# Modulation sums as one-column products on TensorE, squares of x added on VectorE, and x loaded between the weight tiles

## The chip, the cores and the metric

The kernel runs on one core of a Trainium2 chip. The time is the device time of one execution in microseconds (us); less is better. A core has five engines with a program each: TensorE (PE in the profile, its weight loads PEld), VectorE (DVE), ScalarE (ACT), GpSimd (POOL) and SyncE (SP, which here issues every DMA). They meet only through semaphores.

## The reference

Two transformer blocks on 512 rows of width 1024, all in float32. The change is in what stands ahead of the first block's projections. With x of 512 rows and a vector c of 1024 numbers it computes

```python
mod = c @ w_ada[l] + b_ada[l]                    # (1024) @ (1024, 3072)
shift, scale, gate = jnp.split(mod, 3, axis=-1)
h = _rmsnorm(x, norm_g[l]) * (1.0 + scale[:, None, :]) + shift[:, None, :]
proj = h @ w_in[l]                               # (512, 1024) @ (1024, 6152)
# _rmsnorm(x, g) = x * rsqrt(mean(x * x, axis=-1) + 1e-6) * g
# behind it: stick-breaking attention, forgetting attention, gates, and
# x = x + gate[:, None, :] * (merged @ w_out[l]), then the second block
# (differential attention and convolution, cross attention, conv FFN)
```

`shift` and `scale` are needed before the first projection can start; `gate` much later. `w_ada` has 12 MB, of which 8 MB are for `shift` and `scale`.

## The kernel before, in words

Activations are kept transposed: features on the 128 partitions, the 512 rows along the free dimension, in 8 pieces (`X[:, k, :]`, `HH[:, k, :]`). Weights come in "units" of 128x1024 float32 (512 KB) in a fixed order (`UNITS`), through a ring of four buffers `RAW`. A projection's unit is split in two parts: ScalarE copies it to `WH` (rounded to float32r), GpSimd computes the rest `WL = RAW - WH` in four pieces; TensorE makes three products of each piece (high by high, high by low, low by high).

The first 16 units are `w_ada`: `("ada", 1, k)` for scale and then `("ada", 0, k)` for shift, k = 0..7; a unit holds the 128 rows 128k.. of the matrix and 1024 columns. Behind them come `("av", 0..3)`, the first projection's weights. SyncE's program (`sync_program`) issues the loads in the order of `UNITS`; the load of unit j waits until the buffer's last user, unit j-4, is done. For an `ada` unit that is the signal `s_mod`, for others `s_wh` and `s_wl`.

Each engine's order of work is written out by hand. Up to the first projection it is, before the change:

- **VectorE** (`mod_step`): for each `ada` unit `ma = ma + raw * c[k]`, one pass over 128x1024, where c[k] is one number per partition. Eight passes leave a tile whose sum over the partitions is the product with c. Among the last passes stand the norm's small steps (`root_cols`, `root_inverse`, `diag`, `spread_out`).
- **TensorE** (`mod_end`): eight products of a 128x128 piece of `ma` (the stationary operand) with a column of ones, so that the sum over the partitions comes out with one feature per partition. TensorE also adds the squares of x over the features (`sums`: 8 pieces, each a high and a low part, with a constant matrix), and spreads the norm's factor over the partitions (`spread`).
- **ScalarE**: square of x piece by piece, its high part, the root, the `WH` of the four `av` units, and then `HH[:, k, :]`.
- **GpSimd**: the low parts of the eight squares, then the `WL` of the `av` units.

The loads begin with the parameters (`par_sb`, which hold c), half of x, `raw(0)`, the other half, the constants, then three units. After the 16th `ada` unit VectorE makes `mod_out(0, 1)`, and then for each k a tile `tm`, from which ScalarE makes `HH[:, k, :]` and VectorE `HL[:, k, :]`; TensorE's `vproj("a", ...)` uses them k by k.

In the profile an engine's instructions all carry the line of the helper that emits them: L135 matmul, L142 activation, L145 `tt`, L148 `stt`, L153 `ts`, L156 `cp`, L168 DMA. They are told apart by the tiles.

Of the kernel before, what the change touches and what calls it, by code (L numbers as in the profile page):

```python
# [15 lines left out]
P = 128  # L16
# [234 lines left out]
def build(nc, args):  # L251
# [5 lines left out]
    def at(name, shape, dt, offset=None):  # L257
        nb = int(np.prod(shape[1:])) * (2 if dt == BF16 else 4)
        if offset is None:
            offset = off[0]  # L260
            off[0] += (nb + 31) // 32 * 32
        assert offset + nb <= 229344, (name, offset + nb)
        return nc.alloc_sbuf_tensor_at(name, list(shape), dt, offset=offset)
# [62 lines left out]
    SZ = [at(f"sz{i}", [P, T], F32) for i in range(2)]  # L326
    FT = at("ft", [104, T], F32R)
    MA = at("ma", [P, U], F32, a1)
    MA2 = at("ma2", [P, U], F32, a1 + 4096)

    off[0] = a1
    RB = at("rb", [P, T], F32)
# [56 lines left out]
    def sig(name, step=1):  # L389
        signals.append(Signal(name, step))  # L390
        return signals[-1]
# [8 lines left out]

    s_wh, s_wl, s_unit = sig("s_wh"), sig("s_wl"), sig("s_unit")

    s_sq, s_sqha, s_sqhd, s_sqlp, s_sqld, s_sum = (
        sig(n) for n in ("s_sq", "s_sqha", "s_sqhd", "s_sqlp", "s_sqld", "s_sum"))
    s_add, s_root, s_sqrt, s_spread = sig("s_add"), sig("s_root"), sig("s_sqrt"), sig("s_spread")

    s_conr, s_mk, s_mod, s_modp, s_modc, s_gain = (
        sig(n) for n in ("s_conr", "s_mk", "s_mod", "s_modp", "s_modc", "s_gain"))

    s_ht, s_hh, s_hl = sig("s_ht"), sig("s_hh"), sig("s_hl")  # L410
    s_vh, s_vl, s_qh, s_ql, s_kh, s_kl, s_sz = (
# [56 lines left out]
    def tensor_program(pe):  # L468
# [37 lines left out]
        def sums(key, b, ones, p, hs, ls, first, last, n=T):  # L506
            pe.wait_ge(hs, *key)
            pe.mm(PS[b][:, 0:n], con_r(ones), SQh[p][:, 0:n], first, False)
            pe.wait_ge(ls, *key)
            pe.mm(PS[b][:, 0:n], con_r(ones), SQl[p][:, 0:n], False, last).then_inc(*s_sum.up(*key))  # L510
# [17 lines left out]
            bank[b] = (s_modc, (part,))  # L528

        pe.wait_ge(s_conr, 0)
        for k in range(KC):
            sums(("x", k), 7, "o1024", k % 2, s_sqha, s_sqlp, k == 0, k == KC - 1)
        mod_end(1, 0, MA)
        bank[7] = (s_root, ("x", "mult"))
        spread("x", 7, TM[2])
        bank[7] = (s_root, ("x", "out"))
        mod_end(0, 1, MA2)

        def vproj(br, nm, gen):  # L540
            for u in range(4):
# [591 lines left out]
    def lam(a, b):  # L1133
        return LM[:, a:b]
# [38 lines left out]
    def scalar_program(act):  # L1173
# [19 lines left out]

        for k in range(KC):
            act.wait_ge(l_x if k < 4 else l_xb, 0)
            if k == 7:
                act.wait_ge(s_sqlp, "x", 0)
            square(TM[k % 7][:, :], ("x", k), X[:, k, :])
            if k >= 2:
                act.wait_ge(s_sum, "x", k - 2)  # L1200
            act.wait_ge(s_sq, "x", k)
            act.fn(SQh[k % 2][:, :], TM[k % 7][:, :], ACT.Copy).then_inc(*s_sqha.up("x", k))
        act.wait_ge(l_con, 0)
        root("x", ncol("x"))
        for j in range(N_ADA, N_ADA + RING):
# [75 lines left out]

        act.wait_ge(l_mem, 0)
        act.fn(MSQ[:, :, :], MEMT[:, :, :], ACT.Square).then_inc(*s_sq.up("mem"))
        act.wait_ge(s_modp, 0)
        vproj("a", "av", VAh)
        qk_high("a", 0, "q")
        root("mem", ncol("mem", 2))
# [354 lines left out]
    def vector_program(dve):  # L1642
# [54 lines left out]
        dve.wait_ge(l_cont, 0)  # L1697
        dve.cp(conr[:, :], CONT[:, :]).then_inc(*s_conr.up(0))

        def mod_step(part, k, ma):  # L1700
            j = PLACE["ada", part, k]
            dve.wait_ge(l_raw[j % RING], j)
            dve.wait_ge(l_par, 0)
            if k == 0:
                dve.ts(ma[:, :], RAW[j % RING][:, :], pcol("c", k), ALU.mult).then_inc(*s_mod.up(part, k))
            else:
                dve.wait_ge(s_mod, part, k - 1)
                dve.stt(ma[:, :], RAW[j % RING][:, :], pcol("c", k), ma[:, :], ALU.mult,
                        ALU.add).then_inc(*s_mod.up(part, k))

        def mod_out(part, b):
            dve.wait_ge(s_modp, part)
            dve.tt(sm[:, 8 * part:8 * part + 8], PS[b][:, 0:8], prow("b_ada", 8, 8 * part),
                   ALU.add).then_inc(*s_modc.up(part))

        for k in range(KC):
            mod_step(1, k, MA)
        for k in range(KC):
            mod_step(0, k, MA2)
            if k == 1:  # L1720
                mod_out(1, 0)
                root_cols("x", 7, TM[1], ("x", 7))
                root_inverse("x")
            if k == 3:
                diag("x", TM[2], ncol("x"), "x")
            if k == 4:
                spread_out("x", 7, SZ[1][:, :])
        dve.wait_ge(l_msk, 0)
        dve.cp(MK[:, 0:512], MKR[:, 0:512]).then_inc(*s_mk.up(0))
        dve.cp(MK[:, 512:768], MKR[:, 512:768]).then_inc(*s_mk.up(1))  # L1730
        dve.wait_ge(s_modc, 1)
        dve.ts(sm[:, 8:16], sm[:, 8:16], 1.0, ALU.add).then_inc(*s_gain.up("one"))
        dve.wait_ge(s_gain, "one")
        dve.tt(sm[:, 8:16], sm[:, 8:16], prow("norm_g", 8), ALU.mult).then_inc(*s_gain.up("g"))
        mod_out(0, 1)
        dve.wait_ge(s_gain, "g")
        dve.wait_ge(s_root, "x", "out")
        dve.wait_ge(s_modc, 0)
        dve.wait_ge(s_sqlp, "x", 7)
        for k in range(KC):  # L1740
            t = TM[(3 + k) % 7]
            if k == 7:
# [608 lines left out]
    def pool_program(pool):  # L2351
# [15 lines left out]
        def parts(l, src, h, key, s_l):  # L2367
            pool.tt(l, src, f32(h), ALU.subtract).then_inc(*s_l.up(*key))

        for k in range(KC):  # L2370
            pool.wait_ge(s_sqha, "x", k)
            if k >= 2:
                pool.wait_ge(s_sum, "x", k - 2)
            parts(SQl[k % 2][:, :], TM[k % 7][:, :], SQh[k % 2][:, :], ("x", k), s_sqlp)
        for j in range(N_ADA, N_ADA + RING):
            low(UNITS[j])
        for name in UNITS[N_ADA:PLACE["ak", 0] + 1]:
# [63 lines left out]
    def sync_program(sp):  # L2441
        def raw(j):
            s = j % RING
            if j >= RING:
                name = UNITS[j - RING]
                if name[0] == "ada":
                    sp.wait_ge(s_mod, name[1], name[2])
                else:
                    sp.wait_ge(s_wh, name)
                    sp.wait_ge(s_wl, name)  # L2450
            sp.dma(RAW[s][:, :], units[j]).then_inc(*l_raw[s].up(j))
# [6 lines left out]
                sp.dma(gate_tile(k, x)[:, :], gate_w[k, :, T * x:T * x + T]).then_inc(*l_gate[x].up(k))  # L2458

        sp.dma(par_sb[:, :], par).then_inc(*l_par.up(0))  # L2460
        sp.dma(X[:, 0:4, :], xin[:, 0:4, :]).then_inc(*l_x.up(0))
        raw(0)
        sp.dma(X[:, 4:8, :], xin[:, 4:8, :]).then_inc(*l_xb.up(0))
        sp.dma(CONT[:, :], con[:, 0:CO + 8]).then_inc(*l_cont.up(0))
        sp.dma(con_raw[:, :], con[:, CO:NCON]).then_inc(*l_con.up(0))
        for j in range(1, RING):
            raw(j)
        sp.dma(MKR[:, :], msk).then_inc(*l_msk.up(0))
        def keep(n):
            sp.wait_ge(s_gl, n)  # L2470
            sp.dma(kept[n, :, :], GE[n % 3][:, :]).then_inc(*l_kept[n % 3].up(n))
# [12 lines left out]
        for j in range(RING, len(UNITS)):  # L2484
            done = UNITS[j - 2 * RING] if j >= 2 * RING else None
            if done and done[0] == "g":
                keep(2 * (done[1] % 8) + done[1] // 8)
            for k, first in enumerate((0, 2, 5, 7, 10, 12, 14, 15)):
                if j == b0 + first:
                    gate(k)  # L2490
            if j == PLACE["oa", 0] + RING + 3:
                for n in range(6):
                    back(n)
            if j == PLACE["oa", 0] + 2 * RING:
                sp.wait_ge(s_pv, "b", 7)
                sp.dma(X[:, :, :], xin).then_inc(*l_x2.up(0))
            for u in range(3):
                if j == PLACE["ob", u] + 2 * RING + 1:
                    for n in range(4 * u + 6, min(4 * u + 10, 16)):
                        back(n)  # L2500
            if j == PLACE["wo", 0] + 2 * RING:
                sp.wait_ge(s_unit, ("ob", 3))
                sp.dma(CT[:, :].bitcast(I32), posin).then_inc(*l_pos.up(0))
                sp.dma(lam(0, 256), lamin).then_inc(*l_lam.up(0))
            if j == N_ADA + RING:
                sp.wait_ge(s_modc, 0)
                sp.dma(MEMT[:, :, :], memin).then_inc(*l_mem.up(0))
            if j == PLACE[gate_unit(5)] + 2 * RING:
                sp.wait_ge(s_mxl, 3)
                sp.dma(kept_m[0, :, :], f32(MEMh[:, :, :]).rearrange("p k m -> p (k m)")).then_inc(*l_mout[0].up(0))  # L2510
                sp.dma(kept_m[1, :, :], f32(MEMl[:, :, :]).rearrange("p k m -> p (k m)")).then_inc(*l_mout[1].up(0))
            if j == PLACE["dk", 3] + 2 * RING + 1:
                sp.wait_ge(s_unit, ("dk", 3))
                for x, t in enumerate((MTh, MTl)):
                    sp.wait_ge(l_mout[x], 0)
                    sp.dma(f32(t[:, :, :]).rearrange("p k m -> p (k m)"), kept_m[x, :, :]).then_inc(*l_min[x].up(0))
            if j == PLACE["cv", 3, 1] + 2 * RING:
                sp.wait_ge(s_pv, "d", 7)
                for x, (p0, p1) in enumerate(((0, 6), (6, 8))):
                    sp.wait_ge(s_kv, p1 - 1)  # L2520
                    sp.dma(KV[:, p0:p1, :], KVT[:, p0:p1, :]).then_inc(*l_kv[x].up(0))
            raw(j)
# [119 lines left out]
```

## Time and profile before

| | us |
|---|---|
| median of 3 runs | 1446.15 (1442.12 to 1448.85) |
| the profiled execution, its own time | 1445.63 |
| its span, first to last instruction | 1443.8 |
| TensorE matmul busy | 1310.3 (91% of the span) |
| VectorE busy | 793.9 (55%) |
| ScalarE busy | 576.1 (40%) |
| GpSimd busy | 747.8 (52%) |

The span is 1.8 us shorter than the execution's own time. Busy shares are averages over the whole span. The change touches only the stretch ahead of the first projection, some 50 us, and that stretch has to be read by itself.
### The profile page before, as it was taken

The page shows a single profiled execution, that of the slowest core. Times are in us where ns is not written, and L with a number is a line of the kernel's source. Part 1 is how long each engine was busy: PE and PEld are TensorE (multiplying, and loading weights), DVE is VectorE, ACT ScalarE, POOL GpSimd, SP SyncE. Part 2 cuts the span into 40 slices and gives each one's busy share as a digit, 9 for nine tenths or more (in the row PEclk, how much of TensorE's full clock was granted, in tenths as well). Part 3 has the DMA queues.
Part 4 walks back from the last instruction along what each step waited for, and adds up shares of the span by engine and source line. Part 5 has one row for each costly group of instructions (what it writes and reads, how often), then busy time and mean ns, then how long its engine had stood idle before and what let it go on. Part 6 is the DMA issues. An engine that isn't in the chain of part 4 may idle for free.

```text
span 1443.8 us, 17006 instructions
## 1 busy us (share of the span) xinstructions
PE 1310.3 (91%) x6164; PEld 1065.3 (74%) x6164; DVE 793.9 (55%) x1339; ACT 576.1 (40%) x926; POOL 747.8 (52%) x866
## 2 busy tenths in 40 slices
PE   3789999989999899999978788998999999999996
PEld 2567878867888777787656677787878888888874
DVE  5646767423334248796675553775336733661554
ACT  3354555435555236222433453543334423332331
POOL 4353434432333466476233366842556976884771
PEclk9989999999999999999999799999999999999998
DMA  8531223212323642132111334321231333233321
GB/s 298 175 103 51 74 66 124 90 65 92 102 87 111 222 134 95 61 95 95 59 59 44 114 109 144 105 86 44 66 95 61 108 110 97 93 102 101 89 74 58
DMA packets 41699, 142.80 MB, mean 99 GB/s; under 512 B 4624, under 2 KB 5008, under 8 KB 40464
## 3 DMA queue, kind: packets, MB, share of 16 engines
q1 hardware_dynamic: 41616, 141.71, 30.3%
q8 instruction: 49, 0.80, 0.2%
q14 instruction: 34, 0.28, 0.1%
HBM read 131.21 MB, written 8.39 MB: 97 GB/s over the span
## 4 chain that ended last, share of the span: by engine, by line
PE 77%; DVE 12%; ACT 6%; issue 2%; DMA 1%; POOL 0%; SPq 0%; DVEq 0%; ACTq 0%; POOLq 0%
PE ps L135 76%; DVE tm L145 3%; ACT wh L142 2%; ACT tm L142 2%; DVE ma L148 1%; PE ps L139 1%; ACT L142 1%; DVE tm L148 1%; DMA con_raw<-con 1%; ACT hh L142 1%; DVE sql L145 0%; DVE ac L148 0%; DVE x L148 0%; DVE tm L153 0%; DVE stat L159 0%
## 5 line engine op out<-in xcount | busy, mean ns | idle before, releaser
L145 POOL TENSOR_TENSOR wl<-raw,wh 128x256 fp32r<-128x256 f32 x804 | 677.9, 876 | 621.0 <-ACT wh L142 618.8
L142 ACT ACTIVATE wh<-raw 128x1024 fp32r<-128x1024 f32 x201 | 212.2, 1058 | 506.1 <-PE ps L135 494.0
L135 PE MATMUL ps<-hh,wh 128*128 128x512 f32 x872 | 344.7, 395 | 2.8 <-DVE cb L145 1.6
L135 PE MATMUL ps<-hl,wh 128*128 128x512 f32 x872 | 340.6, 391 | 0.0
L135 PE MATMUL ps<-hh,wl 128*128 128x512 f32 x872 | 340.4, 390 | 0.0
L135 PEld LDWEIGHTS ps<-hh,wh 128*128 128x128 f32 x872 | 164.7, 189 | 39.0 <-DVE cb L145 2.4
L135 PEld LDWEIGHTS ps<-hh,wl 128*128 128x128 f32 x872 | 164.2, 188 | 35.1
L135 PEld LDWEIGHTS ps<-hl,wh 128*128 128x128 f32 x872 | 164.4, 189 | 33.5 <-issue 0.5
L148 DVE SCALAR_TENSOR_TENSOR tm<-cb,par_sb,tm 128x512 f32<-128x512 f32 x88 | 87.5, 994 | 50.8 <-ACT tm L142 47.5
L145 DVE TENSOR_TENSOR tm<-tm,tm 128x512 f32<-128x512 f32 (+3 forms) x106 | 91.0, 862 | 35.3 <-ACT tm L142 32.4
L142 ACT ACTIVATE tm<-tm 128x512 f32<-128x512 f32 (+3 forms) x109 | 54.5, 532 | 87.2 <-DVE tm L148 81.6
L145 DVE TENSOR_TENSOR x<-ps,x 128x512 f32<-128x512 f32 x40 | 27.5, 688 | 101.7 <-PE ps L135 101.6
L142 ACT ACT_TABLE_LOAD x50 | 64.2, 1283 | 28.5 <-DVE stat L153 15.2
L135 PE MATMUL ps<-zh,wh 128*128 128x512 f32 x176 | 69.9, 397 | 2.3 <-DVE zh L156 2.3
L135 PE MATMUL ps<-zl,wh 128*128 128x512 f32 x176 | 69.3, 394 | 0.8 <-POOL zl L145 0.8
L135 PE MATMUL ps<-zh,wl 128*128 128x512 f32 x176 | 69.6, 395 | 0.0
L142 ACT ACTIVATE tm<-ps,stat 128x256 f32<-128x256 f32 (+3 forms) x80 | 40.8, 516 | 46.9 <-DVE stat L153 46.8
L148 DVE SCALAR_TENSOR_TENSOR ac<-cpf,par_sb,ac 128x512 f32<-128x512 f32 x60 | 56.5, 941 | 1.6
L159 DVE TENSOR_REDUCE stat<-ps 128x1 f32<-128x256 f32 (+3 forms) x80 | 37.6, 470 | 30.5 <-PE ps L135 30.4
L145 DVE TENSOR_TENSOR cb<-ps,rb 128x512 f32<-128x512 f32 x44 | 30.1, 684 | 28.6 <-PE ps L135 28.5
L142 ACT ACTIVATE tm<-cb,par_sb 128x512 f32<-128x512 f32 x44 | 31.3, 712 | 29.7 <-DVE cb L145 29.6
L135 PE MATMUL ps<-wh,hh 128*128 128x512 f32 x96 | 38.8, 404 | 4.0 <-ACT hh L142 4.0
(316 smaller groups left out, 2414.7 us busy)
## 6 DMA issues: line engine op xcount, KB each, us to landing
raw<-units SPq DMA_DIRECT2D x217, 512.0 KB, 3.5
kept<-ge SPq DMA_DIRECT2D x16, 256.0 KB, 2.0
tm<-kept SPq DMA_DIRECT2D x16, 256.0 KB, 3.7
tm<-gate_w SPq DMA_DIRECT2D x12, 256.0 KB, 4.1
x<-xin SPq DMA_DIRECT2D x2, 1024.0 KB, 6.7
x<-xin SPq DMA_DIRECT2D x1, 2048.0 KB, 12.1
out<-x SPq DMA_DIRECT2D x8, 256.0 KB, 2.2
kv<-kvt SPq DMA_DIRECT2D x1, 1536.0 KB, 7.3
```

Source lines behind the costliest of these rows:

```text
L135: return self.none if self.e is None else self.e.matmul(out, lhs, rhs, start=start, stop=stop, skip_group_check=skip)
L139: return self.none if self.e is None else self.e.transpose(out, in_, ident)
L142: return self.none if self.e is None else self.e.activation(out, in_, func, **kw)
L145: return self.none if self.e is None else self.e.tensor_tensor(out, a, b, op)
L148: return self.none if self.e is None else self.e.scalar_tensor_tensor(out, a, s, b, op0, op1)
L159: return self.none if self.e is None else self.e.tensor_reduce(out, in_, AX_X, op, **kw)
```

## The change

- `mod_step`, `MA2` and two of the three `mod_end` go. In their place TensorE multiplies each `ada` unit directly: eight products per unit, each a 128x128 piece of `RAW` (stationary) with the column c[k] of the parameters (one moving column), summed over k in PSUM (`ada(part, k)`). The signal `s_ada`, given by the last of the eight, is what the reload of the buffer waits for.
- The squares of x are added on VectorE (`add_square`): pieces 0 to 6 into one tile, and the sum and piece 7 are each split in high and low there. TensorE makes four products instead of sixteen, in the middle of the `ada` units. ScalarE keeps only the squares, GpSimd has nothing to do there.
- Units 0 to 3 are loaded earlier, the halves of x between them, and the mask `MKR` comes later, behind unit 17.

```diff
-        pe.wait_ge(s_conr, 0)
+        def ada(part, k):
+            s = PLACE["ada", part, k] % RING
+            pe.wait_ge(l_par, 0)
+            pe.wait_ge(l_raw[s], PLACE["ada", part, k])
+            for f in range(8):
+                last = pe.mm(PS[part][:, f:f + 1], RAW[s][:, f * 128:(f + 1) * 128], pcol("c", k), k == 0 and f == 0,
+                             k == 7, skip=True)
+            last.then_inc(*s_ada.up(part, k))
+
         for k in range(KC):
-            sums(("x", k), 7, "o1024", k % 2, s_sqha, s_sqlp, k == 0, k == KC - 1)
-        mod_end(1, 0, MA)
-        bank[7] = (s_root, ("x", "mult"))
-        spread("x", 7, TM[2])
-        bank[7] = (s_root, ("x", "out"))
-        mod_end(0, 1, MA2)
+            ada(1, k)
+        bank[1] = (s_modc, (1,))
+        for k in range(KC):
+            ada(0, k)
+            if k == 2:
+                pe.wait_ge(s_conr, 0)
+                sums(("x", 6), 7, "o1024", 0, s_sqhd, s_sqld, True, False)
+                sums(("x", 7), 7, "o1024", 1, s_sqhd, s_sqld, False, True)
+                bank[7] = (s_root, ("x", "mult"))
+            if k == 6:
+                spread("x", 7, TM[5])
+                bank[7] = (s_root, ("x", "out"))
+        bank[0] = (s_modc, (0,))
...
         for k in range(KC):
             act.wait_ge(l_x if k < 4 else l_xb, 0)
-            if k == 7:
-                act.wait_ge(s_sqlp, "x", 0)
-            square(TM[k % 7][:, :], ("x", k), X[:, k, :])
-            if k >= 2:
-                act.wait_ge(s_sum, "x", k - 2)
-            act.wait_ge(s_sq, "x", k)
-            act.fn(SQh[k % 2][:, :], TM[k % 7][:, :], ACT.Copy).then_inc(*s_sqha.up("x", k))
+            if k >= 3:
+                act.wait_ge(s_add, "x", k - 2)
+            square(square_tile(k)[:, :], ("x", k), X[:, k, :])
...
         for k in range(KC):
-            mod_step(1, k, MA)
-        for k in range(KC):
-            mod_step(0, k, MA2)
-            if k == 1:
-                mod_out(1, 0)
-                root_cols("x", 7, TM[1], ("x", 7))
-                root_inverse("x")
-            if k == 3:
-                diag("x", TM[2], ncol("x"), "x")
-            if k == 4:
-                spread_out("x", 7, SZ[1][:, :])
+            add_square("x", k, (None, None))
+        root_cols("x", 7, TM[6], ("x", 7))
+        root_inverse("x")
+        diag("x", TM[5], ncol("x"), "x")
         dve.wait_ge(l_msk, 0)
         dve.cp(MK[:, 0:512], MKR[:, 0:512]).then_inc(*s_mk.up(0))
         dve.cp(MK[:, 512:768], MKR[:, 512:768]).then_inc(*s_mk.up(1))
+        mod_out(1, 1)
...
+        spread_out("x", 7, SZ[1][:, :])
+        mod_out(0, 0)
...
                 if name[0] == "ada":
-                    sp.wait_ge(s_mod, name[1], name[2])
+                    sp.wait_ge(s_ada, name[1], name[2])
```

`add_square` stands in the kernel before already, for later norms; it adds `t0 = t0 + t` for f = 1..6 and splits `t0` and the last square in two parts each.

TensorE's program in the kernel before, from the low part of the last square to the second product of the first projection (`ma` and `ma_125` hold the sums for scale and shift, `tm_68` the norm's diagonal; `x8` are the eight pieces):

```order
L135 MATMUL ps<-sql_84,conr 128x512
L135 MATMUL ps<-con_raw,ma 128x1 x8
L135 MATMUL ps<-tm_68,con_raw 128x512
L135 MATMUL ps<-con_raw,ma_125 128x1 x8
L135 MATMUL ps<-wh_53,hh 128x512
L135 MATMUL ps<-wl_57,hh 128x512
```

The same place in the changed kernel, from the third shift unit on (`raw_49` to `raw_52` are the ring's four buffers, `par_sb` holds the column c[k]):

```order
L135 MATMUL ps<-par_sb,raw_51 128x1 x8
L135 MATMUL ps<-sqh_81,conr 128x512
L135 MATMUL ps<-sql_83,conr 128x512
L135 MATMUL ps<-sqh_82,conr 128x512
L135 MATMUL ps<-sql_84,conr 128x512
L135 MATMUL ps<-par_sb,raw_52 128x1 x8
L135 MATMUL ps<-par_sb,raw_49 128x1 x8
L135 MATMUL ps<-par_sb,raw_50 128x1 x8
L135 MATMUL ps<-par_sb,raw_51 128x1 x8
L135 MATMUL ps<-tm_71,con_raw 128x512
L135 MATMUL ps<-par_sb,raw_52 128x1 x8
L135 MATMUL ps<-wh_53,hh 128x512
```

Two groups of eight one-column products stood ahead of the first projection; now sixteen do, eleven ahead of this piece's second row and five behind it.

SyncE's program at the very start, as the difference from before (-) to after (+):

```order
 L168 DMA par_sb<-par 128x374
+L168 DMA raw_49<-units 128x1024
+L168 DMA raw_50<-units 128x1024
 L168 DMA x<-xin 128x2048
-L168 DMA raw_49<-units 128x1024
-L168 DMA x<-xin 128x2048
+L168 DMA raw_51<-units 128x1024
+L168 DMA raw_52<-units 128x1024
 L168 DMA cont<-con 128x776
 L168 DMA con_raw<-con 128x400
```

Two weight units now stand ahead of the first half of x, and only the parameters ahead of them; the second half of x goes behind the constants.

## Rows read from the trace of the kernel before

**Rows 1.** The page: span, and the chain that ended last by engine.

```profile
span 1443.8 us, 17006 instructions
...
PE 77%; DVE 12%; ACT 6%; issue 2%; DMA 1%; POOL 0%; SPq 0%; DVEq 0%; ACTq 0%; POOLq 0%
```

**Rows 2.** Chain in order of time, 0 to 110 us: start, duration, what.

```profile
25.63 2.11 DVE ma L148
27.74 0.04 issue
27.78 3.59 PE ps L135 x16
...
43.54 1.29 DVE ma L148
44.85 4.69 DMA raw<-units
49.56 0.25 ACT wh L142
...
54.20 40.14 PE ps L135 x167
```

**Rows 3.** Timeline from 12 us: start, duration, engine, line, out<-in, [idle <-releaser].

```profile
12.95 0.63 PE L135 MATMUL ps<-sql,conr 128*128 128x512 f32 x1
12.96 0.33 PEld L135 LDWEIGHTS ps<-sqh,conr 128*128 128x128 f32 x1
13.00 32.18 SPq L168 DMA_DIRECT2D raw<-units  x16
13.07 14.65 DVE L148 SCALAR_TENSOR_TENSOR ma<-raw,par_sb,ma 128x1024 f32<-128x1024 f32 x7
13.38 0.63 PE L135 MATMUL ps<-sqh,conr 128*128 128x512 f32 x1
...
27.78 3.49 PEld L135 LDWEIGHTS ps<-con_raw,ma 128*128 128x128 f32 x16 [0.79 <-DVE ma L148]
27.78 3.57 PE L135 MATMUL ps<-con_raw,ma 128*128 128x1 f32 x16 [0.29 <-DVE ma L148]
...
38.08 2.05 PE L135 MATMUL ps<-tm,con_raw 128*128 128x512 f32 x2 [6.72 <-DVE tm L145]
...
44.87 3.57 PE L135 MATMUL ps<-con_raw,ma 128*128 128x1 f32 x16 [4.75 <-DVE ma L148]
...
55.86 0.63 PE L135 MATMUL ps<-wh,hh 128*128 128x512 f32 x1
...
56.28 0.63 PE L135 MATMUL ps<-wl,hh 128*128 128x512 f32 x1
```

**Rows 4.** Instructions writing `ma` or reading it, 20 to 32 us: ns min/median/max.

```profile
L135 PEld LDWEIGHTS ps<-con_raw,ma x16: 288/333/333, 27.8 to 30.9; 128*128 128x128 f32 x16
```

**Rows 5.** Timeline of TensorE at the fast pace, 58 us and 481 us.

```profile
58.70 0.40 PE L135 MATMUL ps<-wl,hh 128*128 128x512 f32 x1
...
58.93 0.40 PE L135 MATMUL ps<-wh,hl 128*128 128x512 f32 x1
...
481.57 1.84 PE L135 MATMUL ps<-con_raw,ma 128*128 128x1 f32 x16
483.27 0.48 PE L135 MATMUL ps<-vah,wh 128*128 128x512 f32 x1
```

**Rows 6.** DMA issues, 0 to 60 us: KB each, median us from issue to landing.

```profile
raw<-units SPq DMA_DIRECT2D x24, 512.0 KB, 4.5
x<-xin SPq DMA_DIRECT2D x2, 1024.0 KB, 6.7
...
par_sb<-par SPq DMA_DIRECT2D x1, 187.0 KB, 2.4
```

**Rows 7.** The page's DMA issues over the whole span.

```profile
raw<-units SPq DMA_DIRECT2D x217, 512.0 KB, 3.5
```

**Rows 8.** Stretches of 2 us: PE, PEld, DVE, ACT, POOL busy, PEclk, DMA share, GB/s.

```profile
4.00:6.00 2.00, 0.00 (x0) 0.00 (x0) 0.00 (x0) 0.00 (x0) 0.00 (x0) 1.00 0.96 395
...
14.00:16.00 2.00, 1.45 (x4) 0.64 (x3) 1.90 (x2) 1.91 (x4) 1.67 (x2) 1.00 1.03 401
...
22.00:24.00 2.00, 1.22 (x2) 0.50 (x2) 1.90 (x2) 0.69 (x2) 2.00 (x2) 1.00 0.77 225
...
40.00:42.00 2.00, 0.12 (x1) 0.00 (x0) 1.84 (x2) 0.00 (x0) 0.00 (x0) 1.00 0.90 324
```

**Rows 9.** VectorE by group, the whole span.

```profile
L145 DVE TENSOR_TENSOR tm<-tm,tm 128x512 f32<-128x512 f32 x81 | 80.2, 995 | 13.5 <-ACT tm L142 10.6
...
L145 DVE TENSOR_TENSOR sql<-tm,sqh 128x512 fp32r<-128x512 f32 x12 | 11.6, 968 | 0.4
...
L156 DVE CAST sqh<-tm 128x512 fp32r<-128x512 f32 x12 | 8.3, 688 | 1.0 <-ACT tm L142 0.8
```

More of the change, by code:

```diff
@@ L328, in build @@
     MA = at("ma", [P, U], F32, a1)
-    MA2 = at("ma2", [P, U], F32, a1 + 4096)
     off[0] = a1
@@ L401, in build @@
     s_wh, s_wl, s_unit = sig("s_wh"), sig("s_wl"), sig("s_unit")
-    s_sq, s_sqha, s_sqhd, s_sqlp, s_sqld, s_sum = (
-        sig(n) for n in ("s_sq", "s_sqha", "s_sqhd", "s_sqlp", "s_sqld", "s_sum"))
+    s_sq, s_sqhd, s_sqld, s_sum = sig("s_sq"), sig("s_sqhd"), sig("s_sqld"), sig("s_sum")
     s_add, s_root, s_sqrt, s_spread = sig("s_add"), sig("s_root"), sig("s_sqrt"), sig("s_spread")
-    s_conr, s_mk, s_mod, s_modp, s_modc, s_gain = (
-        sig(n) for n in ("s_conr", "s_mk", "s_mod", "s_modp", "s_modc", "s_gain"))
+    s_conr, s_mk, s_ada, s_mod, s_modp, s_modc, s_gain = (
+        sig(n) for n in ("s_conr", "s_mk", "s_ada", "s_mod", "s_modp", "s_modc", "s_gain"))
     s_ht, s_hh, s_hl = sig("s_ht"), sig("s_hh"), sig("s_hl")
@@ L1283, in scalar_program @@
         act.fn(MSQ[:, :, :], MEMT[:, :, :], ACT.Square).then_inc(*s_sq.up("mem"))
-        act.wait_ge(s_modp, 0)
         vproj("a", "av", VAh)
@@ L1698, in vector_program, with mod_out @@
         dve.cp(conr[:, :], CONT[:, :]).then_inc(*s_conr.up(0))
-        def mod_step(part, k, ma):
-            j = PLACE["ada", part, k]
-            dve.wait_ge(l_raw[j % RING], j)
+        def mod_out(part, b):
             dve.wait_ge(l_par, 0)
-            if k == 0:
-                dve.ts(ma[:, :], RAW[j % RING][:, :], pcol("c", k), ALU.mult).then_inc(*s_mod.up(part, k))
-            else:
[L1707 to L1712, printed above, removed]
+            if part == 2:
+                dve.wait_ge(s_modp, 2)
+            else:
+                dve.wait_ge(s_ada, part, 7)
             dve.tt(sm[:, 8 * part:8 * part + 8], PS[b][:, 0:8], prow("b_ada", 8, 8 * part),
@@ L1734, in vector_program @@
         dve.tt(sm[:, 8:16], sm[:, 8:16], prow("norm_g", 8), ALU.mult).then_inc(*s_gain.up("g"))
-        mod_out(0, 1)
+        spread_out("x", 7, SZ[1][:, :])
+        mod_out(0, 0)
         dve.wait_ge(s_gain, "g")
@@ L1738, in vector_program @@
         dve.wait_ge(s_modc, 0)
-        dve.wait_ge(s_sqlp, "x", 7)
         for k in range(KC):
@@ L2368, in parts @@
             pool.tt(l, src, f32(h), ALU.subtract).then_inc(*s_l.up(*key))
[L2370 to L2374, printed above, removed]
         for j in range(N_ADA, N_ADA + RING):
@@ L2460, in sync_program @@
         sp.dma(par_sb[:, :], par).then_inc(*l_par.up(0))
+        raw(0)
+        raw(1)
         sp.dma(X[:, 0:4, :], xin[:, 0:4, :]).then_inc(*l_x.up(0))
-        raw(0)
-        sp.dma(X[:, 4:8, :], xin[:, 4:8, :]).then_inc(*l_xb.up(0))
+        raw(2)
+        raw(3)
         sp.dma(CONT[:, :], con[:, 0:CO + 8]).then_inc(*l_cont.up(0))
         sp.dma(con_raw[:, :], con[:, CO:NCON]).then_inc(*l_con.up(0))
-        for j in range(1, RING):
-            raw(j)
-        sp.dma(MKR[:, :], msk).then_inc(*l_msk.up(0))
+        sp.dma(X[:, 4:8, :], xin[:, 4:8, :]).then_inc(*l_xb.up(0))
         def keep(n):
@@ L2504, in sync_program @@
                 sp.dma(lam(0, 256), lamin).then_inc(*l_lam.up(0))
+            if j == N_ADA + 2:
+                sp.dma(MKR[:, :], msk).then_inc(*l_msk.up(0))
             if j == N_ADA + RING:
```

## The prediction, made before the changed kernel ran

> **What bounds the kernel now.** The page comes first: TensorE makes up 77% of the chain that ended last, VectorE 12% [rows 1]. That is the whole span, and the change touches its first 50 us, so the next view is the chain in order of time from 0 to 110 us. There TensorE isn't the engine that sets the end. The chain runs over VectorE's passes on `ma` (the last of the first eight at 25.63), over one group of 16 one-column passes on TensorE (27.78, 3.59 us), over VectorE's passes again up to 44.83, then over the load of the last `av` unit (44.85, 4.69 us) and ScalarE's copy of it at 49.56. From 54.20 on TensorE has 167 matmuls in one piece [rows 2]. So what the first stage costs the kernel is read off one event: the moment from which TensorE runs the first projection without a gap, 54.20. All that follows hangs on that, and shifts with it.
>
> The timeline shows why VectorE takes so long: seven passes in 14.65 us, of which the last takes 2.11 where one of the second eight takes 1.29 [rows 2, 3]. GpSimd is busy beside the long ones (2.00 of 2 us at 22 to 24) and idle beside the short ones (0.00 at 40 to 42) [rows 8]. The load isn't the limit: the DMA engines moved 395 to 401 GB/s at 4 to 6 and 14 to 16 us, and 225 at 22 to 24, when a free buffer was what they lacked [rows 8].
>
> **The clock.** PEclk reads 1.00 in these stretches [rows 8], since no change is on record ahead of 58.42. The pace says something else: consecutive 512-column passes start 0.43 us apart at 12.95 and 13.38 [rows 3], against 0.23 at 58.70 and 58.93 [rows 5]. So TensorE runs at 1.2 GHz in the stage that the change alters, and at 2.4 GHz from 58.4 on.
>
> **What goes.** VectorE's 16 passes over `raw` and the two groups of `ma` products leave the path. GpSimd's eight low parts and ScalarE's eight copies go too; neither is in the chain.
>
> **What comes on TensorE.** The new product has exactly the form of the old one in `mod_end`: a 128x128 float32 piece loaded, one column moved. Its price is in the trace. Eight products are 16 passes, loaded in 3.49 us with the last load taking 0.288, hence (3.49 - 0.288) / 15 = 0.2135 us from one pass to the next [rows 3, 4]. At 2.4 GHz, at 481.57, the 16 take until 483.27: 1.70 us, 0.106 a pass [rows 5]. The price is that of the weight load; the single column costs nothing beside it. A unit so costs 16 x 0.2135 = 3.42 us at the slow clock, against 1.29 to 2.11 us on VectorE. That is the heart of the forecast: the change takes the sum from an engine that needs 1.3 us for a unit to one that needs 3.4, and all 16 units stand in TensorE's own order ahead of the first projection.
>
> The Trainium skill (TensorE: Matmul & The Clock Gate, section "LDWEIGHTS (loading the stationary operand)") gives a load as columns divided by 1.2 GHz, which is 107 ns for 128 columns. By that a unit would cost 1.7 us at the low clock. The trace has 213 ns a pass for this float32 form [rows 3, 4], twice the page's figure, and the measurement decides.
>
> **The sum**, as the time at which the 16th unit is done:
> - Start. The parameters landed 2.4 us after their issue at about 0.74 [rows 6], so 3.1 is the earliest. They and the first unit are 0.7 MB; 0.4 MB/us from about 3 us [rows 8] puts the landing at 4.7. The late end is 6.5: a first half of x of 1 MB, behind the parameters, had 6.7 us as median from issue [rows 6], and this load is half of that. I take 4.7.
> - 256 passes at 0.2135: 54.7.
> - The four products for the squares, in the middle: 4 x 0.43 = 1.7 [rows 3].
> - The spread, now ahead of the 16th unit: 2.05 [rows 3].
>
> 4.7 + 54.7 + 1.7 + 2.05 = 63.2. Before, VectorE was done with the 16th unit at 44.83.
>
> From there the path is as before: the buffer's reload, `WH`, `HH`, TensorE. The load took 4.69 us among others in flight [rows 2]; in the changed kernel the three units ahead of it were issued 3.4 us or more apart, so it finds the queue empty. I take the median of all, 3.5 [rows 7]; the ends are 2.4 (187 KB, an easier load) and 4.7 [rows 6, 2]. From the landing at 49.56 to the gapless 54.20 it was 4.64 us [rows 2], over ScalarE's copy, two rounds of `HH` and `HL` and GpSimd's `WL` beside them. GpSimd's work on this last unit still runs beside these rounds, so I leave 4.64. The new moment is 63.2 + 3.5 + 4.64 = 71.3, against 54.20: **17.1 us later**.
>
> **What is hidden.** VectorE's part of the squares is six additions, two casts and two subtractions: 6 x 0.995 + 2 x 0.69 + 2 x 0.97 = 9.3 us [rows 9]. The second half of x is the ninth load; the bytes up to it are 5.0 MB, 12.5 us at 0.4 MB/us behind 3 us, so VectorE has the parts by about 22 us. TensorE wants them after 11 units: 4.7 + 11 x 3.42 = 42.3. The cover is 20 us. The root's steps begin after 44.0 and take some 5 us; the spread wants them after the 15th unit, at 57.7. The mask's load goes out at the 14th unit's end, 54.3, and with 4.5 us to land and VectorE's two casts it is done by 60, ahead of the 16th unit. If it were later it would hold up `mod_out`, which stands behind it on VectorE. Behind SyncE's new wait on `s_ada` stand only later units, each needing its own buffer, and memory's load, which needed this point before as well.
>
> Beyond the first projection nothing is changed, and I cost it at zero. TensorE again starts it at the low clock: neither kernel has dense work directly before it. In before the clock rose 4.2 us after 54.20; the same work may get it 2 us earlier or later.
>
> The profiled execution took 1445.63, 0.5 under the median. 1445.63 + 17.1 = 1462.7; on the median 1463.2. I say 1463. About 7 us, 0.5%, is what a measurement here can tell from no change.
>
> **Rival A, faster: the clock rises during the one-column products.** Then a unit costs 1.70, and the eight products follow each other for tens of microseconds without a gap, more than any stretch in the trace of before. By the rule of the Trainium skill (TensorE: Matmul & The Clock Gate, Part 1) sustained TensorE activity releases the throttle; its Part 4 says of transposes that they don't count as busy in the same way, and of one-column products it says nothing. What the trace shows: dense 512-column work from 54.20 reached the fast clock 4.2 us later, while two groups of one-column passes, 3.57 us each and gapless, at 27.78 and 44.87, left it low: 512-column passes behind the second, at 55.86 and 56.28, still start 0.42 apart, and no rise is on record ahead of 58.42 [rows 3]. 3.57 is less than 4.2, so they don't settle it; but they come close. At the price: 4.7, then 4.2 us at the low clock (1.2 units), 14.8 x 1.70 = 25.2, four passes at 0.23, a spread at half, 1.0: done at 36.0. With 3.5 + 4.64 gapless from 44.1, 10.1 us earlier: 1436. The loads would be nearly in the way (11.3 MB at 0.4 MB/us are 28 us, and a buffer comes round after 3 x 1.7 = 5.1 us where a load has a median of 4.5 [rows 6]), so 1436 to 1440. This becomes the case from the point at which the fast clock holds over more than about 10 of the 16 units: 17.1 / (3.42 - 1.70) = 10.
>
> **Rival B, half of it: the clock rises only after the squares' products**, which are the sole 512-column work in the middle, and stays for the last five units: 5 x 1.72 + 1.0 saved, 1454. Against it: eight such pairs of passes at 12 to 27 us with gaps didn't raise it either, and here are only four passes.
>
> **Rival C, slower still: each unit pays an uncovered start.** Every eight products begin behind a wait for a load. If that costs the length of one load, 0.33, and the tail of one pass, 0.1, each time, the sum grows by 16 x 0.43 = 7: 1470. For it: the group at 27.78 shows 3.57 rather than 3.42 for 16 passes. Against it: the loads are long there when TensorE asks (a buffer comes round after 10.3 us against 4.5), so the next unit's first weights can be fetched while the last is running.
>
> **Rival D, no change:** the late start is given back later, because GpSimd and ScalarE are ahead with the next units' parts when the first projection starts. Against it: the 167 matmuls behind 54.20 are one piece without a wait [rows 2], so there is nothing there to give back.
>
> **How the numbers follow.** The forecast has 0.80, rival A 0.08, B 0.03, C 0.06, D 0.03. Own range of the forecast: start -1.6 to +1.8, landing -1.1 to +1.2, clock of the projection 2 either way, the runs of before -4 to +3; taken together about 1456 to 1469. The range reaches to B and C on its two sides: 1454 to 1470. Below it lies A. Faster by over 0.5% is A, 0.08; within 0.5% is D and a weak form of B, 0.04; slower the rest, 0.88.
>
> **What would show it.** In the changed kernel's timeline: groups of 16 one-column passes 3.4 us apart from about 5 us, the last ending near 63; VectorE idle for the most part between 22 and 44; the load of the last `av` unit issued near 63 and landed in 3.5; the first gapless matmul near 71; PEclk with no rise recorded ahead of 75. DMA at some 150 GB/s (0.52 MB per 3.4 us) between 20 and 60. The forecast is wrong if the passes come 0.107 apart (rival A), if a group's first load stands apart from the last group's end (C), or if TensorE waits for loads between the groups, which none of the above holds.

## The result, and the profile after

| | before | after |
|---|---|---|
| median, us | 1445.75 (4 runs) | 1464.2 (4 runs, 1461.51 to 1471.46) |
| the profiled execution | 1445.63 | 1462.25 |
| its span | 1443.8 | 1460.5 |
| TensorE's gapless stretch begins | 54.20 | 71.73 |
| from there to the end of the span | 1389.6 | 1388.8 |

The change made the kernel slower: ratio 1.0136, 95% interval 1.0091 to 1.0182. The forecast was 1463, slower. The four runs of the changed kernel lie 10 us apart, so the medians can't tell the forecast from one a few microseconds off; the start of the gapless stretch can.

The page after, its head and the new group of instructions, which answers to [rows 1]:

```profile
span 1460.5 us, 17388 instructions
...
PE 80%; DVE 11%; ACT 6%; issue 2%; DMA 1%; POOL 0%; DVEq 0%; ACTq 0%; SPq 0%; POOLq 0%
...
L135 PE MATMUL ps<-par_sb,raw 128*128 128x1 f32 x256 | 54.7, 351 | 5.7 <-DMA raw<-units 5.7
```

The chain in order of time, after (start, duration, what), which answers to [rows 2]:

```profile
1.18 4.42 DMA raw<-units
5.60 0.14 issue
5.74 58.17 PE ps L135 x262
63.91 0.02 issue
63.93 3.36 DMA raw<-units
67.29 0.02 issue
67.31 0.02 ACT wh L142
...
71.73 39.74 PE ps L135 x167
```

Before, the chain went over VectorE, TensorE, VectorE, a load. Now one piece of 58.17 us on TensorE fills it: 256 one-column passes, 4 of the squares and 2 of the spread. Then comes the load, 3.36 us, and 4.44 us to the gapless stretch, which is 17.5 us later than before. Behind it the two executions take the same to 0.8 us. So the loss lies wholly ahead of the first projection.

The timeline after (start, duration, engine, line, out<-in, [idle <-releaser]), which answers to [rows 3]:

```profile
5.74 37.68 PE L135 MATMUL ps<-par_sb,raw 128*128 128x1 f32 x176 [5.74 <-DMA raw<-units]
...
43.28 0.77 PE L135 MATMUL ps<-sqh,conr 128*128 128x512 f32 x1
...
45.37 0.69 DVE L145 TENSOR_TENSOR tm<-ps,con_raw 128x512 f32<-128x512 f32 x1 [23.00 <-PE ps L135]
...
58.64 2.05 PE L135 MATMUL ps<-tm,con_raw 128*128 128x512 f32 x2
...
60.18 1.66 DVE L156 CAST mk<-mkr 128x512 bf16<-128x512 f32 x2 [10.79 <-DMA mkr<-msk]
...
60.48 3.41 PE L135 MATMUL ps<-par_sb,raw 128*128 128x1 f32 x16
```

A group of eight products takes 3.41 us. 176 passes start between 5.74 and 43.28: 0.2133 us each, where the passes of `mod_end` in the kernel before gave 0.2135. VectorE waited 23.0 us for the squares' products: it had its parts at 22.4, where the chain needs them at 43.3.

Stretches of the kernel after: PE, PEld, DVE, ACT, POOL busy, PEclk, DMA share, GB/s (to [rows 8]):

```profile
24.00:32.00 8.00, 8.00 (x40) 8.00 (x39) 0.00 (x0) 0.00 (x0) 0.00 (x0) 1.00 0.54 160
32.00:40.00 8.00, 8.00 (x39) 8.00 (x39) 0.00 (x0) 0.00 (x0) 0.00 (x0) 1.00 0.47 164
```

### The profile page after: what moved, and what is told of

Same layout as the page of the kernel before. It is cut to its first block, busy times and chain, and to the rows that moved or that the text cites. A ratio compares the mean times of both kernels' runs of the same rounds, so it can differ in the third digit from the quotient of the medians.

```text
span 1460.5 us, 17388 instructions
## 1 busy us (share of the span) xinstructions
PE 1350.1 (92%) x6376; PEld 1110.3 (76%) x6376; DVE 773.7 (53%) x1333; ACT 571.6 (39%) x918; POOL 732.8 (50%) x858
## 4 chain that ended last, share of the span: by engine, by line
PE 80%; DVE 11%; ACT 6%; issue 2%; DMA 1%; POOL 0%; DVEq 0%; ACTq 0%; SPq 0%; POOLq 0%
PE ps L135 79%; DVE tm L145 3%; ACT wh L142 2%; ACT tm L142 1%; PE ps L139 1%; DVE tm L148 1%; ACT L142 1%; DMA raw<-units 1%; ACT hh L142 0%; DVE sql L145 0%; DVE ac L148 0%; DVE x L148 0%; DVE tm L153 0%; DVE atl L145 0%; DVE stat L159 0%
## 5 line engine op out<-in xcount | busy, mean ns | idle before, releaser
L145 DVE TENSOR_TENSOR tm<-tm,tm 128x512 f32<-128x512 f32 (+3 forms) x112 | 95.1, 852 | 36.1 <-ACT tm L142 32.8
L135 PEld LDWEIGHTS ps<-par_sb,raw 128*128 128x128 f32 x256 | 55.2, 333 | 6.9 <-issue 6.7
L135 PE MATMUL ps<-par_sb,raw 128*128 128x1 f32 x256 | 54.7, 351 | 5.7 <-DMA raw<-units 5.7
```

The costliest lines, as they stand in the source:

```text
L135: return self.none if self.e is None else self.e.matmul(out, lhs, rhs, start=start, stop=stop, skip_group_check=skip)
L145: return self.none if self.e is None else self.e.tensor_tensor(out, a, b, op)
```

## The experiments

Ten kernels ran, in three rounds. Every one is read by two numbers: its median with the ratio to the kernel before on the same chip, and the start of the gapless stretch in its profile. The rounds ran on different chips, so ratios and gapless starts are compared across rounds rather than medians. The edits are shown shortened: several lines may be written as one, and loads as a list in their order.

| kernel | gapless from | median | ratio, 95% interval |
|---|---|---|---|
| before | 54.20 | 1445.75 to 1446.52 | |
| changed | 71.73 | 1464.2 | 1.0136 (1.0091 to 1.0182) |
| e1, sums on VectorE | 56.22 | 1451.2 | 1.0029 (1.0006 to 1.0052) |
| e2, squares as before | 76.09 | 1470.66 | 1.0155 (1.0119 to 1.0191) |
| e3, row products | 56.78 | 1450.89 | 1.0032 (1.0011 to 1.0053) |
| e4, dense work first | 71.42 | 1466.89, one run | |
| e5, row products, loads moved | 52.09 | 1445.71 | 0.9992 (0.9977 to 1.0007) |
| e6, shared by two engines | 50.78 | 1446.62 | 1.0001 (0.9988 to 1.0015) |
| e7, as e1, loads moved | 53.09 | 1450.15 | 1.0027 (1.0015 to 1.0039) |
| e8, as e5, HH first | 49.89 | 1444.69 | 0.9973 (0.9958 to 0.9988) |
| e9, as e8, four units on VectorE | 55.99 | 1450.39 | 1.0012 (0.9996 to 1.0028) |
| e10, loads only | 59.34 | 1449.88 | 1.0023 (1.0009 to 1.0038) |

One of the twelve executions of e7 took 6459 us, for a reason that nothing on record shows; without it the median is 1450.03.

**e1, the products undone.** The changed kernel with `mod_step` and `mod_end` back.

```diff
-        for k in range(KC): ada(1, k)        # TensorE, one-column products
+        for k in range(KC): mod_step(1, k, MA)   # VectorE
+        mod_end(1, 1, MA)
...
+        dve.cp(conr[:, :], CONT[:, :])       # now behind the first eight passes
```

> The changed kernel with the products put back on VectorE (16 passes over the units, then one-column products of their sums), the squares and the loads as changed, and the copy of the constants behind the first eight passes. Theory (the one-column products at the low clock are the whole loss): VectorE starts at 5.7, passes take 1.3 since GpSimd is idle, 5.7 + 10.3 + 0.6 + 8 for the squares + 8 x 1.4 + 3 for the root = 38.8; with 3.5 to land and 4.64 the gapless stretch begins near 47, against 54.2 before and 71.7 after: about 1439 us. Rival (the new order of the loads is at fault): it stays near 1460.

Measured: gapless from 56.22, median 1451.2. So 15.5 of the 17.5 us lost come back with the products alone (and the copy of the constants, which had to move with them); the rival, the loads' order, can't account for the loss. The forecast of 47 for the gapless stretch was 9 us too early, though. The timeline of e1:

```profile
6.91 1.28 DVE L148 SCALAR_TENSOR_TENSOR ma<-raw,par_sb,ma 128x1024 f32<-128x1024 f32 x1 [1.26 <-DMA raw<-units]
...
17.22 5.45 DVE L148 SCALAR_TENSOR_TENSOR ma<-raw,par_sb,ma 128x1024 f32<-128x1024 f32 x4 [3.87 <-DMA raw<-units]
...
47.62 1.57 DVE L156 CAST mk<-mkr 128x512 bf16<-128x512 f32 x2 [3.85 <-DMA mkr<-msk]
```

VectorE's passes take 1.28 each with GpSimd idle, where they took 2.11 beside GpSimd's work before, but they wait for units that stand behind x and the constants, and at the end for the mask. An engine that needs 1.3 us per unit feels the loads' order; one that needs 3.4 doesn't.

**e2, the squares undone.** ScalarE's and GpSimd's split of the eight squares back, 16 products on TensorE.

```diff
         for k in range(KC):
             ada(1, k)
+            if k >= 3: square_sum(k - 3)     # and behind ada(0, 0..2)
```

> The changed kernel with the squares of x made as before: split by ScalarE and GpSimd, 16 products on TensorE, two behind each of eight units, instead of VectorE's additions and 4 products. Theory (only TensorE's own order counts in this stage): 12 passes more at 0.43 us, so 5.2 us above the changed kernel, about 1468. Rival (VectorE's additions are part of the loss): at or below the changed kernel, 1463 or less.

Measured: 1470.66, gapless from 76.09, which is 4.4 us behind the changed kernel's. The 12 passes more would be 5.1 us; this execution's first unit landed 0.9 earlier (4.84 against 5.74). TensorE's own order decides, as theory had it: its piece in the chain is 63.29 us, against 58.17 in the changed kernel. So the squares part of the change is a gain of about 5 us inside a larger loss. This is read from the traces; the ratios, 1.0155 and 1.0136, have intervals that overlap.

**e3, the operands swapped.** The same numbers are multiplied in a form in which the unit is the moving operand.

```diff
-            for f in range(8):
-                pe.mm(PS[part][:, f:f + 1], RAW[s][:, f * 128:(f + 1) * 128], pcol("c", k), ...)
+            for x in range(2):
+                pe.mm(PS[2 * part + x][0:1, :], pcol("c", k), RAW[s][:, x * T:(x + 1) * T], k == 0, k == 7)
```

> The changed kernel with the operands swapped: the column of c is stationary (one column), the unit streams through in two pieces of 512 columns, and the row that comes out is turned to columns by eight one-column products. [...] Theory (the clock stays low because one column moves per product): the clock rises within some 4 us of the start, a unit then takes 1.7 instead of 3.4, the 16th is done near 39, the gapless stretch begins near 47, about 1439 us. Rival (in this stage nothing raises the clock, or the cost is TensorE's whatever the form): the unit stays at 3.4 us and the time near 1463.

Its timeline at the start and in the middle, and the turned row at the end:

```profile
5.57 5.56 PE L135 MATMUL ps<-raw,par_sb 128*1 128x512 f32 x8 [5.57 <-DMA raw<-units]
...
19.77 4.45 PE L135 MATMUL ps<-raw,par_sb 128*1 128x512 f32 x10
...
49.06 3.57 PE L135 MATMUL ps<-con_raw,ma 1*128 1x1 f32 x16 [5.93 <-DVE ma L156]
```

A unit is 4 passes of 512 columns. From 19.77 on ten passes take 4.45 us, a pass itself 0.59, so they start 0.43 us apart: a unit takes 1.72 and the clock is high. In this form a unit goes through twice as fast, a pace which the one-column form didn't reach in 58 us. The rival that nothing can raise the clock in this stage falls. The median, 1450.89, was again over the forecast of 1439, and the last row shows the largest part of it: the 16 passes that turn the second row start at 49.06, 5.93 us after TensorE's last work. VectorE's copies of that row stood behind its casts of the mask, and the mask had landed at 44.7. By then the clock had fallen (PEclk reads 0.50 from 48 us on) and these passes cost 3.57 instead of 1.9.

**e4, dense work first.** Does the clock hold, once raised?

```diff
+        for n in range(6):                   # 512 columns of a constant tile
+            pe.mm(PS[6][:, :], TM[6][:, 0:128], TM[6][:, :], True, True)
         for k in range(KC):
             ada(1, k)
```

> The changed kernel with six float32 products of 512 columns on a constant tile ahead of the units, from about 1.5 to 11 us, to raise the clock first. Theory (one-column products neither raise nor hold the clock): the first few units run at 0.107 a pass, then the passes fall back to 0.213 and stay there; the stage ends about 11.5 - 5.7 = 5.8 us later less some 2 to 6 us for the fast passes. Rival (a busy TensorE holds a clock once raised): all 16 units at 1.7 us, the 16th done near 42, gapless near 50.

Stretches of e4: PE busy, PEclk, DMA share, GB/s. Dense passes until 8.4, one-column passes from then on:

```profile
5.00:8.40 3.40, 3.40 (x10) 1.00 1.00 396
8.40:11.80 3.40, 3.40 (x32) 0.99 1.01 412
11.80:15.20 3.40, 3.40 (x17) 0.50 1.04 429
15.20:18.60 3.40, 3.40 (x17) 0.50 0.99 388
```

The clock rose, 32 one-column passes ran in 3.40 us at 0.99, and from 11.8 on 17 did in the same time at 0.50. TensorE was busy for 3.40 of 3.40 us throughout. So one-column products didn't hold the clock here, as they didn't raise it in the changed kernel, though the engine shows no gap; the profile's busy share says nothing about that. This is the piece that the prediction couldn't settle from the trace of before. It is one execution, but from 11.8 to the end of the stage at 63.4 PEclk reads 0.50. The dense work itself cost nothing here: two units' worth of fast passes repaid it, and the stage ended at 63.4 against 63.9.

**e5, e6 and e7, with the loads and the mask placed for a faster stage.**

```diff
-        raw(0), raw(1), X[:, 0:4], raw(2), raw(3), CONT, con_raw, X[:, 4:8]
+        raw(0), raw(1), raw(2), raw(3), X[:, 0:4], CONT, con_raw, raw(4), raw(5), X[:, 4:8]
...
-        dve.cp(MK[:, 0:512], MKR[:, 0:512])  # both casts now behind the making of HH and HL
```

> The row products of e3 (column of c stationary, the unit streamed) with all four first units ahead of x, the second half of x behind the sixth unit, and the mask's load and VectorE's two casts of it moved behind the making of HH. In e3 TensorE waited 3.3 us for loads, and VectorE waited until 44.7 for the mask, ahead of the copies of the second row. Theory (the loss of the changed kernel is the slow clock, and what e3 kept of it is the mask's and the loads' waits): 5 + 3.4 + 15 x 1.72 + 0.9 + 1.1 + 1.9 = 38 to 40 for the 16th unit, gapless near 48, about 1440 us. Rival (e3's remainder is TensorE's): gapless stays at 57, about 1449.

> As e5, with every second unit given to VectorE (8 passes of 1.3 us) and the others to TensorE's row products (8 x 1.7), both parts added in PSUM by one-column products; ScalarE copies the rows. Theory: no engine is then the bound but the loads, 11.3 MB at 0.4 MB/us, so the 16th unit is done at 31 to 34, gapless near 41 to 43, about 1434 us. Rival (with the engine half idle the clock falls again, or waits between the engines add up): 16th unit near 40, about 1440.

> The sums on VectorE as in e1 (no products on TensorE), with the loads and the mask placed as in e5. In e1 VectorE waited 7.6 us for units and 3.9 for the mask. Theory: 5 + 16 x 1.3 + 0.6 + 8 + 3 = 37 to 39 for the 16th unit, gapless near 47, about 1439 us, so that VectorE alone is as good as TensorE at the fast clock. Rival (it is the loads that end this stage, in any order): gapless stays at 54 to 56, about 1446 to 1449.

e5's gapless stretch begins at 52.09, 4.7 us ahead of e3's, and its median is that of the kernel before: the mask and the loads, which this run moves together, were part of the remainder but not all of it, since 48 was expected. Its chain:

```profile
12.63 7.37 DMA raw<-units
20.05 21.66 PE ps L135 x62
41.73 5.93 DMA raw<-units
...
52.09 40.55 PE ps L135 x167
```

Up to 20 us the loads bound it, in the middle TensorE, and then the last `av` unit, which took 5.93 us with others in flight where 3.5 were assumed.

e6 gave every second unit to VectorE. The forecast of 41 to 43, from the loads alone, failed (50.78). Stretches of e6:

```profile
20.00:26.00 6.00, 5.71 (x8) 0.58 0.74 256
...
42.00:46.00 4.00, 3.80 (x19) 0.51 0.43 172
```

After a wait of 4.1 us for a unit the clock fell, and PEclk reads 0.50 from 15 to 25; it fell again at 35.3, behind 32 one-column passes, and at 42.1, among the next 32. TensorE's last unit was done at 38.2, against 41.7 in e5 with twice as many. An estimate from these stretches: the busy time spent at the low clock (15.3 us at half pace) added some 7.7 us to TensorE's work, and TensorE waited 12.0 us for units, where it waited 7.3 in e5. So both parts of the named rival came, the fallen clock and the waits; how they share the loss this run can't say.

e7 has VectorE alone, with no products of units on TensorE. Gapless from 53.09, not 47, because VectorE still waited for units:

```profile
14.63 2.67 DVE L148 SCALAR_TENSOR_TENSOR ma<-raw,par_sb,ma 128x1024 f32<-128x1024 f32 x2 [3.77 <-DMA raw<-units]
19.68 2.67 DVE L148 SCALAR_TENSOR_TENSOR ma<-raw,par_sb,ma 128x1024 f32<-128x1024 f32 x2 [2.38 <-DMA raw<-units]
```

Its median, 1450.15, is 4 us above the kernel before although the stretch begins 1.1 us earlier. What adds those 5 us isn't ahead of the projection, and I come back to it below.

**e8 and e9, towards a better kernel.**

```diff
-        for j in range(N_ADA, N_ADA + RING): hi(UNITS[j])
+        for j in range(N_ADA, N_ADA + RING - 1): hi(UNITS[j])
         for k in range(KC):
+            if k == 2: hi(UNITS[N_ADA + RING - 1])
             act.fn(HH[:, k, :], ...)
```

> e5 with ScalarE making HH of pieces 0 and 1 ahead of its copy of the last av unit, and the mask's load later still. In e5 the last av unit landed 5.9 us after the 16th unit, HH(0) came at 48.64, although its input was there at 46.2. Theory (the tail between the 16th unit and the first projection is bound by that load): gapless 2.4 us earlier than in e5, near 49.7, about 1443 us. Rival (the projection waits for the last unit all the same): unchanged, 52, 1445.7.

> e8 with four of the 16 units (k = 1 and 3 of each half) summed on VectorE. TensorE has 4 x 1.72 = 6.9 us less and two groups of one-column products more, 3.8: the 16th unit about 3 us earlier than in e8, gapless near 47, about 1440 us. Rival (the loads are the bound by then): as e8.

The mask's load, which in e5 was issued right behind that of the last `av` unit, goes four units later as well; the edit above leaves this out, and its share is not separated. e8 does what was said: `HH[:, 0, :]` comes at 46.22, against 48.64 in e5, and the gapless stretch begins at 49.89; median 1444.69, ratio 0.9973 (0.9958 to 0.9988). It is the one kernel here that beats the kernel before, by 0.3%; its median lies 19.5 us under that of the changed kernel. The chain of e8 no longer holds the load of the last `av` unit behind the 16th unit, but the copy of the row and its turning:

```profile
19.95 21.68 PE ps L135 x62
41.66 1.29 DVE ma L156 x2
42.99 1.96 PE ps L135 x16
...
49.89 39.56 PE ps L135 x167
```

e9 took four units away from TensorE and got slower (55.99). Stretches of e9:

```profile
30.00:35.00 5.00, 5.00 (x35) 1.00 0.89 308
37.00:41.00 4.00, 4.00 (x17) 0.50 0.43 135
41.00:44.50 3.50, 3.50 (x5) 0.50 0.00 0
```

TensorE's groups in e9, the first two of one-column passes, then a third and a row unit behind it:

```profile
31.51 1.95 PE L135 MATMUL ps<-con_raw,md 128*128 128x1 f32 x16
33.39 1.94 PE L135 MATMUL ps<-con_raw,ma 1*128 1x1 f32 x16
...
37.57 3.58 PE L135 MATMUL ps<-con_raw,md 128*128 128x1 f32 x16
41.08 3.57 PE L135 MATMUL ps<-raw,par_sb 128*1 128x512 f32 x4
```

From 31.5 to 35.3 TensorE ran 32 one-column passes back to back, from 37.6 on 16 more; from 36.5 to 46.7 the clock is low (0.50), and one row unit takes 3.57 us instead of 1.9. In e5 and e8 one group of 16 between two units left the clock high. The 16th unit was done at 48.5, against 41.6 in e8. An estimate of the difference: 6.8 us from passes at the low clock (two stretches, 16.0 to 19.4 and 36.5 to 46.7, at half pace), 3.2 from longer waits for units (10.6 against 7.4), 3.8 for the groups of one-column products, less 6.9 for the four units. So the fallen clock is the largest part and not the whole; that other places for the groups would have kept the clock is not shown.

**e10, only the loads.** The kernel before with the changed kernel's order of loads.

```diff
-        X[:, 0:4], raw(0), X[:, 4:8], CONT, con_raw, raw(1), raw(2), raw(3), MKR
+        raw(0), raw(1), X[:, 0:4], raw(2), raw(3), CONT, con_raw, X[:, 4:8]   # MKR behind raw(17)
```

> The kernel before with nothing but the changed kernel's order of loads. VectorE's first instruction there is the copy of the constants, which then land at about 14.3 instead of 11.7; its passes follow one another from there to the end of the stage. Theory: the whole chain 2.6 to 3 us later, gapless near 57, about 1448.5 us. Rival (units that are there earlier make up for it): no change.

Gapless from 59.34, 5.1 us later; median 1449.88. What VectorE waited for in e10, 40 to 60 us (us in total, times, longest):

```profile
DVE mk L156 <- DMA mkr<-msk: 5.1, 1, 5.1
```

The constants came 1.5 us later (VectorE's first cast 13.26 instead of 11.74), and VectorE then stood 5.1 us for the mask with `mod_out` behind it. I had foreseen the first and missed the second. By itself this part of the change is a loss of 5.1 us at the gapless stretch and of 3.4 us in the medians (1.3 to 5.5 by the interval); in the changed kernel TensorE's 58 us cover it.

## Why the prediction was right, step by step

- **Start of the products:** 4.7 forecast, 5.74 measured. The first unit landed 4.4 us after its issue at 1.18; the loads of half of x and of three more units had been issued by then.
- **256 passes at 0.2135:** 54.7 forecast. 0.2133 a pass measured, hence 54.6 as against 54.7. The sum's largest term was right because the operation's exact form stood in the trace of before, at the same clock. The forecast that the clock stays low was right. The prediction had it from two short groups and gave the other outcome 0.08, without a test of its own; e3 and e4 show that it is the form of the products that leaves it there.
- **Squares and spread:** 1.7 and 2.05 forecast. 43.28 to 45.13 and 58.64 to 60.48: 1.85 and 1.84.
- **The 16th unit:** 63.2 forecast, 63.91.
- **The last load and the way to the projection:** 3.5 and 4.64 forecast, 3.36 and 4.44 measured [rows 2].
- **Gapless from** 71.3 forecast, 71.73 measured: 17.5 us later, where 17.1 were forecast. The misses of the terms, +1.0 and -0.6, half cancel.
- **Nothing beyond:** 1389.6 and 1388.8 us from there to the end.
- **The median** moved by 18.45, 1.4 more than forecast. With four runs 10 us apart, that closeness is partly luck; the gapless stretch isn't.
- **What was hidden** was hidden, but in one place barely. VectorE's squares were ready at 22.4 (22 forecast). The mask was to be done by 60, ahead of the 16th unit. It landed at 60.18; casts, `mod_out(1)`, the gain and the copy of the spread ran to 63.74, and the 16th unit was done at 63.91. A margin of 0.2 us, where I had counted three or more: the sum had the landing and the casts, and left out the 2.0 us of small steps behind them. With a faster stage it became the bound, as e1 and e3 show, and e10 in the kernel before.
- **The rivals:** A (the clock rises) was refuted in the profile (0.2133 a pass to the end) and by e4 in its reason. B didn't happen (3.41 us for the last unit, behind the squares and the spread). C neither: the groups follow each other without a gap (3.41 us per 16 passes). D fell with e1, where the time came back at the place.

The profile's sign named for the clock, no rise on record ahead of 75, held: the passes of 512 columns start 0.43 us apart up to 74.66 and 0.23 from 75.64 on, which is some 3.4 to 3.9 us into the gapless stretch (4.2 before).

**What stays open.** At the level of 2 to 5 us the medians don't follow the gapless stretch alone: e7 begins it 1.1 us before the kernel before and is 4 us slower, e1 begins it 2 us later and is 5 us slower. From that point to the end the profiled executions took 1387.0 us (e5) to 1398.1 (e1). Most of it goes with the clock: over 19 runs of the kernel before, a straight line gives 1.1 us for each 0.001 of the mean granted clock, and they range from 0.959 (1450.7 us) to 0.966 (1442.5). Read against such a line through the runs of the kernel before on the same chip, that is, at the same mean clock, the runs of e1 are 3.1 us slower (2.0 by the gapless stretch), those of e2 22.0 (21.9), those of e7 1.0 (-1.1) and those of e10 3.2 (5.1). What is left beside the clock is about 2 us either way. The row kernels can't be read so: PEclk shows a low stretch of theirs ahead of the projection (47 to 57 us in e5) where it reads 1.00 in the kernel before, and that alone lowers their mean. Why e7's runs had a lower clock (median 0.960 against 0.963 for before on that chip) no experiment here explains.

## What to carry to other kernels

Before moving a matrix-vector product to TensorE, find a product of the same form in the trace and multiply: here, with 128 columns loaded for one moved, the price was that of the weight load, 3.41 us a unit at the low clock. Where it has to be there, let the large operand move and the vector stand still: a unit then cost the same at the high clock (1.72 us against 1.70), and the clock rose. Even so the gain over VectorE was 0.3% in the best kernel. And a stage that gets faster uncovers the order of its loads: look for what stands just behind the old bound (here a mask that TensorE first used at 97 us in the kernel before, 52 us after its casts had begun).

## What the runs showed of the hardware

- TensorE at 100% busy in the profile, for 58 us on end, without reaching the high clock (the changed kernel); and from the high clock, with no gap, back to the low one at 11.8 us, while 32 passes in 3.40 us became 17 (e4). The busy share and the clock are two things.
- Sharing the units between two engines (e6) lost TensorE the high clock: it fell after a wait of 4.1 us for a unit and read 0.58 at 20 to 26 us.
- VectorE's pass over a unit took 1.28 us with GpSimd idle (e1) and 2.11 beside GpSimd's work (before, and e10).
- Passes of 512 float32 columns, each behind a load of one column, start 0.43 us apart at the high clock (e3), against 0.23 for float32r passes [rows 5]. The load of 128 float32 columns goes with the clock: 0.213 us a pass at the low one, 0.106 at the high one.
